# Modulation pages of a fused two-block kernel: later start, products on GpSimd, sums on ACT

## The reference

```python
mod = silu(c) @ ada_w + ada_b                       # 1024 -> 6 * 1024
shift1, scale1, gate1, shift2, scale2, gate2 = split(mod, 6)
h = rms_norm(x, norm1_gain) * (1 + scale1) + shift1
r_q, r_k, r_v, r_g, s_q, s_k, s_v = split(h @ w_in, 7 x 512)
y_ret = head_group_norm(retention(r_q, r_k, r_v)) * silu(r_g)   # r_q, r_k rotated by position
y_sb  = rms_norm(stick_breaking(rms_norm(s_q), rms_norm(s_k), s_v))
x = x + gate1 * (concat(y_ret, y_sb) @ w_out)
h2 = rms_norm(x, norm2_gain) * (1 + scale2) + shift2
x = x + gate2 * peer(h2)                             # 16384 single-neuron experts, all computed densely
```

## Time and profile before

| | us |
|---|---|
| median of 3 runs | 1312.9 |
| the profiled execution's own time | 1317.64 |
| its span | 1315.8 |
| PE busy | 1271.0 (97%) |
| DVE busy | 988.0 (75%) |
| ACT busy | 727.2 (55%) |
| POOL busy | 301.3 (23%) |

### The profile page before, as it was taken

How to read it: one execution, slowest core, us unless ns; L and a number is a source line. 1 busy time by engine, 2 the same in 40 slices (tenths; PEclk the granted TensorE clock), 3 DMA queues, 4 the chain that set the end, 5 groups by cost and what they waited for, 6 DMA issues and landing times.

```text
span 1315.8 us, 19970 instructions
## 1 busy us (share of the span) xinstructions
PE 1271.0 (97%) x7982; PEld 1139.2 (87%) x7982; DVE 988.0 (75%) x1712; ACT 727.2 (55%) x1131; POOL 301.3 (23%) x186
## 2 busy tenths in 40 slices
PE   5999979999999999998999999999989998999999
PEld 5778869999999999998888888888878687899997
DVE  5879998899999789994777777777775466755555
ACT  3565544555555599993554444455555456554443
POOL 0126010277866888540000000000000013000000
PEclk8989989999999999999999999999989998999999
DMA  9954669967777768889887878787645432455552
GB/s 370 368 213 159 209 255 368 313 192 233 241 239 231 229 190 282 278 299 351 317 308 277 304 275 307 273 303 278 234 164 180 163 132 105 150 180 195 184 193 94
DMA packets 138878, 317.11 MB, mean 241 GB/s; under 512 B 24991, under 2 KB 71456, under 8 KB 132898
## 3 DMA queue, kind: packets, MB, share of 16 engines
q1 hardware_dynamic: 101698, 265.42, 56.5%
q10 hardware_dynamic: 14016, 33.56, 6.7%
q0 software_dynamic: 23072, 16.86, 6.6%
HBM read 280.61 MB, written 35.20 MB: 240 GB/s over the span
## 4 chain that ended last, share of the span: by engine, by line
PE 87%; DMA 5%; DVE 4%; SPq 2%; ACT 1%; issue 1%; DVEq 0%; ACTq 0%
PE ps L669 11%; PE ps L671 11%; PE ps L670 11%; PE ps L681 11%; PE ps L682 11%; PE ps L683 11%; PE ps L647 3%; PE ps L648 3%; PE ps L649 3%; DMA wring<-in_w_in 2%; PE ps L966 1%; PE ps L1018 1%; DVE w_lo L1722 1%; DMA peer_arena<-gates_of_second 1%; SPq L523 1%; PE ps L809 1%
## 5 line engine op out<-in xcount | busy, mean ns | idle before, releaser
L1722 DVE TENSOR_TENSOR w_lo<-wring,w_hi 128x1024 fp32r<-128x1024 f32 (+1 forms) x404 | 492.4, 1224 | 183.8 <-ACT w_hi L1250 182.1
L1250 ACT CAST w_hi<-wring 128x1024 fp32r<-128x1024 f32 (+1 forms) x404 | 417.7, 1042 | 258.3 <-PE ps L671 154.8
L669 PE MATMUL ps<-hT_hi,w_hi 128*128 128x256 f32 x1344 | 376.1, 280 | 1.2 <-DVE w_lo L1722 1.2
L671 PE MATMUL ps<-hT_hi,w_lo 128*128 128x256 f32 x1344 | 375.5, 279 | 0.0
L670 PE MATMUL ps<-hT_lo,w_hi 128*128 128x256 f32 x1344 | 375.5, 279 | 0.0
L1674 POOL DMA_INDIRECT gates_of_second<-late x128 | 243.4, 1901 | 126.8 <-issue 50.8
L670 PEld LDWEIGHTS ps<-hT_lo,w_hi 128*128 128x128 f32 x1344 | 255.1, 190 | 0.3
L669 PEld LDWEIGHTS ps<-hT_hi,w_hi 128*128 128x128 f32 x1344 | 252.6, 188 | 1.5 <-issue 1.3
L671 PEld LDWEIGHTS ps<-hT_hi,w_lo 128*128 128x128 f32 x1344 | 253.2, 188 | 0.0
L681 PE MATMUL ps<-w_hi,a_hi 128*128 128x512 f32 x624 | 244.2, 391 | 4.5 <-DVE w_lo L1722 4.5
L683 PE MATMUL ps<-w_hi,a_lo 128*128 128x512 f32 x624 | 243.8, 391 | 0.0
(11 more groups left out here) (326 smaller groups left out, 1504.9 us busy)
## 6 DMA issues: line engine op xcount, KB each, us to landing
wring<-in_peer_down SPq DMA_DIRECT2D x32, 2048.0 KB
wring<-in_peer_up SPq DMA_DIRECT2D x32, 2048.0 KB
wring<-in_w_in SPq DMA_DIRECT2D x11, 2048.0 KB
pages<-in_ada_t POOLq DMA_DIRECT2D x32, 512.0 KB, 5.8
acts_by_expert<-pages ACTq DMA_DIRECT2D x32, 512.0 KB, 3.3
peer_arena<-acts_by_expert SPq DMA_DIRECT2D x32, 512.0 KB, 8.6
wring<-in_w_up SPq DMA_DIRECT2D x8, 2048.0 KB
wring<-in_w_down SPq DMA_DIRECT2D x8, 2048.0 KB
```

Of the source, the lines that this page charges most:

```text
L669: pe.matmul(o, hi[:, k, :], hT_hi[:, k, :], start=(k == 0), stop=False)
L671: mm = pe.matmul(o, lo[:, k, :], hT_hi[:, k, :], start=False, stop=(k == KC - 1))
L1250: act.copy(split_part(kind, w_hi, u, width(kind, j)), part_of(kind, wring[:, n % RING, :], u, width(kind, j))).then_inc(split_hi, 1)
L1722: dve.tensor_tensor(lo, part_of(kind, wring[:, n % RING, :], u, width(kind, j)), hi, ALU.subtract)\
```

## The change

- POOL waits until the fourth chunk has landed (`w_in_slot[1]` at 32) before it issues the first page.
- Of the 32 pages, 12 stay with DVE (numbers 4 to 7 and 24 to 31, `BY_VECTOR`). The other 20 (`BY_PAIRS`) are multiplied in place by POOL (one TENSOR_TENSOR of 128x1024 per page) and summed in place by ACT (a Copy with an accumulator). POOL's and ACT's programs get these at written places.
- A page's place is free when ACT, or DVE, has summed what was in it; POOL's waits follow.
- The decay table and the retention gain move behind the fourth chunk in SP's queue and share one semaphore (`ld_tables`) with the small tables; two other semaphores are merged too.
- On DVE, `late_modulation(1)` now stands before the split of parts 2 and 3 of the first `wq` chunk, with the sums ahead of it gone.

PE's instructions and their order are the same.

```diff
-PAGES_FIRST = 12
-PAGES_BETWEEN = 13
+BY_VECTOR = [*range(4, 8), *range(24, 32)]
+BY_PAIRS = [k for k in range(len(LATER_TILES)) if k not in BY_VECTOR]
@@ sync
             weights(RING)
-            sp.dma_start(spare[:, :], a["decay"]).then_inc(ld_decay, 16)
-            sp.dma_start(rgain, a["ret_gain"].partition_broadcast(P)).then_inc(ld_decay, 16)
             weights(RING + 1)
+            sp.dma_start(spare[:, :], a["decay"]).then_inc(ld_tables, 16)
+            sp.dma_start(rgain, a["ret_gain"].partition_broadcast(P)).then_inc(ld_tables, 16)
@@ scalar
+            def sum_pages(first, last):
+
+                for k in range(first, last):
+                    act.wait_ge(S["page_made"], BY_PAIRS.index(k) + 1)
+                    v, j = PAGES[k % PLACES], LATER_TILES[k]
+                    act.activation(v, v, ACT.Copy, accum_out=modc[:, j:j + 1]).then_inc(S["page_sums"], 1)
...
             take_win(R_Q)
+            sum_pages(0, 2)
             copy_round(1, qT.rearrange("p c t -> p (c t)"))
+            sum_pages(2, 4)
             split("win", S_V, parts=[0])
...
             split("win", R_V, parts=[0])
+            sum_pages(8, 11)
             weight_exp(0)
...
             split("win", R_G, parts=[0, 1])
+            sum_pages(11, 14)
             weight_exp(1)
...
+            sum_pages(16, 18)
             take_values("ret_y", 1, 0, 0, "ret_y_out")
+            sum_pages(18, 20)
             take_win(R_G)
             h_round(2, only=0)
...
             split("wout", 1, parts=[0, 1])
+            sum_pages(20, 22)
             h_round(2, only=1)
@@ gpsimd
             def page(k):
 
+                last = k - PLACES
                 if k < PLACES:
                     pool.wait_ge(S["ada_summed"], k + 1)
+                elif last in BY_VECTOR:
+                    pool.wait_ge(S["ada_summed"], BY_SUMS + BY_VECTOR.index(last) + 1)
                 else:
-                    pool.wait_ge(S["ada_summed"], BY_SUMS + k - PLACES + 1)
+                    pool.wait_ge(S["page_sums"], BY_PAIRS.index(last) + 1)
...
+            def multiply(first, last):
+
+                for k in range(first, last):
+                    pool.wait_ge(page_in[k % PLACES], 16 * (k // PLACES + 1))
+                    v = PAGES[k % PLACES]
+                    pool.tensor_tensor(v, v, s_row, ALU.mult).then_inc(S["page_made"], 1)
...
-            pool.wait_ge(w_in_slot[1], 16)
-            for k in range(PAGES_FIRST):
-                page(k)
+            pool.wait_ge(w_in_slot[1], 32)
+            pages_in(0, 4)
+            pool.wait_ge(S["silu_c"], 1)
+            multiply(0, 4)
+            pages_in(4, 12)
+            multiply(8, 11)
...
                 own(pool.tensor_tensor(rot[1], src[:, :, 0, :], sin, ALU.mult))
+                if b == 0:
+                    pages_in(12, 15)
+                else:
+                    pages_in(16, 18)
                 pool.tensor_tensor(dst[:, :, 1, :], dst[:, :, 1, :], rot[1], ALU.add).then_inc(S["rot_ready"], 1)
                 if b == 0:
-                    for k in range(PAGES_FIRST, PAGES_BETWEEN):
-                        page(k)
-            for k in range(PAGES_BETWEEN, len(LATER_TILES)):
-                page(k)
+                    multiply(11, 14)
+                    page(15)
+            multiply(14, 18)
+            pages_in(18, 20)
+            multiply(18, 20)
+            pages_in(20, 24)
+            multiply(20, 24)
+            pages_in(24, len(LATER_TILES))
@@ vector
             split("win", S_V, parts=[0])
-            sum_pages(2)
+            sum_pages(4, 8)
             split("win", S_V, parts=[1])
...
-            sum_pages(1)
             h_round(3, gain=column(modc, M_SCALE2), shift=column(modc, M_SHIFT2), only=0)
+            late_modulation(1)
             split("wq", 0, parts=[2, 3])
-            sum_pages(3)
-            late_modulation(1)
             h_round(3, gain=column(modc, M_SCALE2), shift=column(modc, M_SHIFT2), only=1)
-            sum_pages(4)
+            sum_pages(24, 28)
             split("wq", 1)
```

More of the change, by code:

```diff
@@ L1785, in _, with take_columns @@
             scales(1, NB, D, 2)
-            def take_columns(first, last, count):
+            def take_columns(first, last, count, pages=0):
                 cols = slice(first, last)
                 dve.wait_ge(S["ada_summed"], count)
+                if pages:
+                    dve.wait_ge(S["page_sums"], pages)
                 return dve.tensor_tensor(modc[:, cols], modc[:, cols], adab[:, cols], ALU.add)
@@ L1803, in sum_tile, with sum_pages @@
                     .then_inc(S["ada_summed"], 1)
-            pages_summed = itertools.count()
-            def sum_pages(n):
-                for _ in range(n):
-                    k = next(pages_summed)
+            def sum_pages(first, last):
+                for k in range(first, last):
                     dve.wait_ge(page_in[k % PLACES], 16 * (k // PLACES + 1))
@@ L1910, in _ @@
             sb_norm(0)
[L1911 to L1915 removed]
+            split("win", R_Q, parts=[1, 2, 3])
             head_squares(2, 3, 5)
@@ L1943, in _ @@
             copy_round(2, kT.rearrange("p c t -> p (c t)"))
-            sum_pages(3)
-            own(take_columns(M_GATE1, M_GATE1 + KC, BY_SUMS + KC))
+            own(take_columns(M_GATE1, M_GATE1 + KC, BY_SUMS + 4, 4))
             dve.sem_inc(S["gate_cols"], 1)
             def late_modulation(half):
-                first, count = half * KC // 2, BY_SUMS + (half + 2) * KC
-                take_columns(M_SHIFT2 + first, M_SHIFT2 + first + KC // 2, count)
-                own(take_columns(M_SCALE2 + first, M_SCALE2 + first + KC // 2, count))
+                first, count = half * KC // 2, KC // 2 + (half + 1) * KC
+                take_columns(M_SHIFT2 + first, M_SHIFT2 + first + KC // 2, BY_SUMS + 4, count)
+                own(take_columns(M_SCALE2 + first, M_SCALE2 + first + KC // 2, BY_SUMS + 4, count))
                 modulation(half + 3, M_SCALE2, G_2, first, KC // 2)
```

62 lines of the change are left out of this document (24 added, 38 removed).

## The result

The changed kernel takes 1338.03 us (median of 4 runs, 1331.13 to 1339.53), beside 1312.49 us for the kernel before on the same chip: the ratio is 1.0178, with a 95% interval of 1.0145 to 1.021. By the ratio it is slower by some 23 us, by the medians by 25.5. I had forecast 1318.5 us and a range that ended at 1326. The sign was right, the size was not: the time lies above the range, and above the rival in which every place came out at its upper end (1326.7).

The account below looks back on a forecast made before the run. PE, with 87% of the chain, was taken as the bound, DVE nearly as full. Terms 0 + 3 + 6 - 3.4 = +5.6 us on the median of 1312.9 gave 1318.5 us; range 1303 to 1326.

Parts of the forecast that it names:

- the rival in which every place came out at its upper end: All four places cost their most, +13.8 us: 1326.7 us; chance 0.15, shared with the fourth chunk not landing sooner.
- What POOL's products cost DVE: DVE and POOL alternate by whole instructions; a caught DVE instruction waits up to 2.36 us, 0 to 47 us over 20 pages.
- rival 2: Whole kernel: gain and loss cancel, each product catching at most one DVE instruction; -0.6 us, 1312.3 us; chance 0.20.
- (a) the start: Near 57 to 76 us: earlier scaling saves 6.1 us uncaught, 2.3 us later if all caught; taken as 0.
- the seven other products: POOL's products outside the four priced places: cost nothing by themselves, covered by freed DVE time and PE's 13 us of matmuls.
- (b) the rotation: Near 126 us: POOL's added products and transfers make PE late by 1.8 to 5.5 us; taken as +3.
- PE for line 1699 near 128 us: Sign at the rotation: PE would newly wait there for POOL's line 1699; no size given.
- (c) the retention output: From 151 to 162.5 us: four products push DVE's gapless chain by 0 to 9.4 us; taken as +6.
- PE for line 2020: Sign at the retention output: PE would newly wait for DVE's line 2020 near 170 us; no size given.
- (d) after x1: Near 194 us: three DVE sums go, modulation precedes two splits, PE's waits of 2.2 and 1.2 us vanish; -3.4.
- Rival 1: Whole kernel: products find gaps, the start gains 6.1 us and the place after x1 3.4; -9.5, 1303.4 us; chance 0.27.

Follow-up runs that it names:

- wait behind each product: The changed kernel with POOL waiting behind each of its 20 page products until it has counted: 1326.7 us, ratio 1.0097.
- one wait per half: The changed kernel with one POOL wait more in each half of the rotation, behind the addition of line 1699: 1326.24 us, ratio 1.0106.
- small stop: The changed kernel with POOL setting 16 scratch columns to zero and waiting for that, ahead of line 1699 in each half: 1323.78 us, ratio 1.0081.
- no products: The changed kernel without POOL's multiplication of 20 pages by silu(c), all transfers, waits and ACT's sums kept: 1307.87 us, ratio 0.9948.
- the stages with turns: Parts of a separate kernel storing zeros, DVE against POOL alone, in which the two alternated: DVE 3.35 us, POOL 3.32 us; no whole-kernel time.

## Why the prediction was wrong

The loss of 1.78% falls into three parts, by the ratios:

| part | from | ratio | us of 1312.9 |
|---|---|---|---|
| DVE passed over by whole rows | changed, less the three kernels with stops (wait behind each product, one wait per half, small stop: 1.0081 to 1.0106) | 0.0072 to 0.0097 | +9.5 to +12.7 |
| the products otherwise: turns with DVE, POOL's own time | these, less no products (0.9948) | 0.0133 to 0.0158 | +17.5 to +20.7 |
| all the rest of the change | no products | -0.0052 (-0.0082 to -0.0021) | -6.8 (-10.8 to -2.8) |

The first two parts are differences of two ratios with intervals of 0.3% to each side, so each is uncertain by some 0.4%, or 6 us. Both lie clear of zero. By the middle values the second is the larger, but that is not shown.

**The step that failed** is the one in "What POOL's products cost DVE" and in rival 2: "each product can catch at most one DVE instruction", so that a caught one "waits up to 2.36 us". It came from rows in which POOL waits for its own semaphore between any two instructions (0.08 us from an end to the next start). The change puts POOL instructions behind each other, and behind a transfer's issue, without such a stop, and there a DVE instruction waited 8.55 and 10.77 us beyond its own 1.22. No row of the trace of before has that order, so the bound "up to 2.36 us" was a bound of another situation. The Trainium skill's rule that I cited (SBUF — State Buffer, section "Who interferes with whom"), that whoever starts first keeps the port for a whole instruction, holds in the stages with turns (products of 3.32, DVE of 3.35 us); it does not hold behind a transfer's issue, where by the record DVE had begun up to 0.41 us first and lost. There the measurement decides.

**(a) the start, forecast 0.** The mechanism was right: the fourth chunk landed near 57 us, the page transfers went out at 57.93, the scaling (64.23) was caught and took 3.33 us, PE's first turn came without a wait. The term was mis-sized: with the stops PE is 2.6 to 5.9 us late at line 830. In the changed kernel PE then waited 3.2 us for DVE's copy of the turned keys (line 1754, behind two caught splits), ran on at half clock (0.50 from 76 to 80 us), and waited up to 3.2 us for the masks. About 3.6 us of the miss is there without products too: I had given the start 6.1 us uncaught, and without products 2.5 were left at line 830. I had called the seven other products, and the sums for pages 4 to 7, free; but DVE waited for those pages, for ACT's cast behind four page sums, and the products of 91 to 99 us stretched (1.29 to 4.49 us) the masks on which the logarithms rest:

```profile
87.23 1.23 DVE L1846 SCALAR_TENSOR_TENSOR pages<-pages,arena 128x1024 f32<-128x1024 f32 x1 [4.46 <-DMA pages<-in_ada_t]
...
95.16 4.49 DVE L1926 TENSOR_TENSOR arena<-arena,const 128x512 f32<-128x512 f32 x2
```

**(b) the rotation, forecast +3.** With stops 2.1 to 2.9 us (line 830 to the second 767). The size is right, but by luck, since my path was wrong: POOL's longer row between the halves did not make the second half late. In the changed kernel POOL still sat idle 5.15 us ahead of it, waiting for DVE's masks, and the wait I had named, PE for line 1699 near 128 us, is in no trace. The loss came through DVE: PE waits for lines 1926 and 1764. In the changed kernel the passed-over splits added 3 us here and 9 to 11 us right behind it, up to line 699, where I had no term at all.

**(c) the retention output, forecast +6.** 6.1 us in the changed kernel, 5.3 to 7.3 with stops, 0.0 without products. The size is right. The wait I had named, PE for line 2020, shows with a wait behind each product and with the small stop (3.0 us each). In the changed kernel PE waited 4.5 us for a split (line 1764) in this stretch instead, and ran on slowly behind it, so there the size was met by another path.

**(d) after x1, forecast -3.4.** From the second line 888 to line 669: -5.4 in the changed kernel, -3.0 to -5.4 with stops, -4.4 without products. Right, a little small.

So the sum of my four terms, +5.6, stands against +8.5 to +11.2 in the kernels with stops, which is the change that I had priced; the other 10 to 13 us of the trace are the rows in which DVE got no turn. The range ended at 1326, just where the kernels with stops lie (1323.8, 1326.2 and 1326.7 us); for a row that gives no turn it had no room.

Rival 1, in which the products cost nothing, is nearest to the kernel without products: 1303.4 forecast, 1307.9 measured. None of the rivals had a DVE instruction that waits for more than one product.

## What to carry to other kernels

Work moved from VectorE to GpSimd is paid on VectorE again where both have the next instruction ready: here 20 products of 2.36 us took 17.5 to 20.7 us, for 23 us of sums saved. Where GpSimd issues a transfer and computes right behind it, let it wait for that first computing instruction before it goes on: a VectorE instruction that comes in the wrong moment then loses one instruction (2.74 us in all) and not the whole row (9.77 and 11.99 us). Two such waits took back as much as twenty. A small instruction with a wait for it between issue and computing (0.2 us) also removed the long ones, but whether by the stop or by the delay is not shown. And a bound read from a trace holds for the order in which its rows stand: before using it, ask whether the instructions around it will still stand, and wait, the same way.

## What the runs showed of the hardware

- In these traces DVE and POOL take turns by whole instructions (3.35 and 3.32 us instead of 1.22 and 2.35), with one exception. A DVE instruction that began 0.01 to 0.41 us ahead of a POOL instruction standing directly behind a transfer's issue (0.01 to 0.02 us from end to start) was passed over until POOL first waited for its own work: 15.30 us behind six products, 10.32 to 10.72 behind four, 11.29 behind eight of half the size. At 0.55 us ahead it kept its turn (1.22), and so it did 0.18 us ahead of a POOL instruction before which POOL had waited (1.22). A wait that is already met does not help (10.72).
- What is blocked: two SBUF operands of 128x1024, and also a TENSOR_SCALAR of 128x16 with one (9.67 us; in turns 1.74 and 2.31 us instead of 0.17). What was not: copies from PSUM (0.69), and two-operand instructions beside POOL's memsets (1.22) or its issuing of transfers (four in 4.63).
- A DVE instruction's duration in the trace includes its wait for POOL, with no idle time shown before it. The sign is a duration above the usual one for its line, not a gap.
